# Gate logits of a two-layer decoder step: eight matmuls dealt out to four column groups of TensorE, and one matmul that adds their sums

## The reference, cut to what matters

```
z = jnp.einsum('btd,dn->btn', x, w_in) + b_in            # x: tokens x 1024
g_nsa = z[..., 1280:1304]                                # 24 of the columns: 8 heads x 3 branches
...
g = jax.nn.sigmoid(gl.astype(jnp.float32))               # gl = g_nsa
o = g[..., 0:1] * o_c + g[..., 1:2] * o_s + g[..., 2:3] * o_w
```

## Time and profile before

| | us |
|---|---|
| median of 3 runs | 1488.45 |
| lowest, highest | 1485.69, 1492.51 |
| the profiled execution, its own time | 1487.74 |
| its span, first to last instruction | 1486.0 |
| TensorE busy in the span | 1413.0 (95%) |
| VectorE busy | 342.0 (23%) |
| ScalarE busy | 307.9 (21%) |
| mean granted TensorE clock | 0.987 |

### The profile page before, as it was taken

The page is one execution under the profiler, slowest core; times in us unless marked ns, Lnnn a source line. Parts: engine busy times, 40 slices in busy tenths (PEclk is TensorE's granted clock), DMA queues, the critical chain, the costliest instruction groups (busy, mean ns, idle before and its releaser), DMA issues.

```text
span 1486.0 us, 23750 instructions
## 1 busy us (share of the span) xinstructions
PE 1413.0 (95%) x9098; PEld 1141.8 (77%) x9098; DVE 342.0 (23%) x887; ACT 307.9 (21%) x811; POOL 158.9 (11%) x268
## 2 busy tenths in 40 slices
PE   7999988999999999999999998899999999999996
PEld 4677767777769977777987777677776898777796
DVE  1222132344422311000122222324442221110002
ACT  1112242244310311000121223313432021100003
POOL 2100325000000000000300123420000000000000
PEclk9999999999999999999999999899999999999998
DMA  9999535596653666565945654467667447556640
GB/s 277 253 240 212 182 99 139 170 315 211 210 200 135 208 213 237 182 215 199 251 151 182 182 158 153 127 182 246 227 199 248 171 141 255 197 186 220 214 145 32
DMA packets 212771, 288.38 MB, mean 194 GB/s; under 512 B 14186, under 2 KB 201788, under 8 KB 211388
## 3 DMA queue, kind: packets, MB, share of 16 engines
q1 hardware_dynamic: 193573, 190.25, 42.8%
q10 hardware_dynamic: 9047, 71.53, 12.9%
q0 software_dynamic: 10048, 25.19, 6.4%
HBM read 277.03 MB, written 72.49 MB: 235 GB/s over the span
## 4 chain that ended last, share of the span: by engine, by line
PE 84%; SPq 5%; DMA 4%; DVE 3%; issue 2%; ACT 2%; DVEq 0%; ACTq 0%
PE psum L1632 76%; PE psum L1636 8%; DMA w_ring<-in_w_in 3%; SPq L506 1%; DMA yT<-in_cache_nsa_kv 1%; SPq L553 1%; SPq L578 1%; SPq L533 1%; SPq L521 0%; DVE pt L1503 0%; DVE logit L1394 0%; SPq L494 0%; SPq L501 0%; ACT xT L1213 0%; DVE logit L1559 0%
## 5 line engine op out<-in xcount | busy, mean ns | idle before, releaser
L1632 PE MATMUL psum<-arena,w_ring 128*128 128x144 f32 (+3 forms) x3584 | 679.5, 352 | 4.0 <-DVE arena L1610 2.3
L1632 PEld LDWEIGHTS psum<-arena,w_ring 128*128 128x128 f32 x3584 | 577.5, 190 | 106.7 <-issue 6.5
L1632 PE MATMUL psum<-xT,w_ring 128*128 128x288 f32 (+1 forms) x1472 | 362.4, 399 | 5.3 <-ACT kt L1152 3.1
L1632 PEld LDWEIGHTS psum<-xT,w_ring 128*128 128x128 f32 x1472 | 264.4, 190 | 79.5 <-issue 10.5
L1610 DVE TENSOR_TENSOR arena<-arena 128x288 f32 x64 | 29.3, 458 | 195.9 <-ACT arena L1225 195.9
L1225 ACT ACTIVATE arena<-psum 128x288 f32<-128x288 f32 x64 | 26.3, 411 | 193.3 <-PE psum L1632 193.3
L892 POOL TENSOR_TENSOR arena<-arena 128x144 f32<-128x144 f32 x24 | 11.7, 489 | 442.4 <-DVE arena L1605 441.3
L1636 PE MATMUL psum<-ident,regrouped 128*128 128x128 f32 x364 | 56.6, 287 | 1.8 <-ACT regrouped L945 1.4
L1636 PEld LDWEIGHTS psum<-ident,regrouped 128*128 128x128 f32 x364 | 45.0, 148 | 7.3 <-issue 3.2
L1306 DVE COPY arena<-psum 128x512 f32<-128x512 f32 x58 | 39.9, 690 | 32.4 <-PE psum L1636 30.7
L1614 DVE SCALAR_TENSOR_TENSOR arena<-arena,psum 128x288 f32<-128x288 f32 x12 | 4.9, 451 | 183.7 <-PE psum L1632 183.7
(11 more groups left out here) (248 smaller groups left out, 1170.8 us busy)
## 6 DMA issues: line engine op xcount, KB each, us to landing
w_ring<-in_w_ff SPq DMA_DIRECT2D x64, 1024.0 KB, 5.4
w_ring<-in_w_in SPq DMA_DIRECT2D x44, 1024.0 KB, 7.2
out<-in_cache_dil_w ACTq DMA_DIRECT2D x8, 1984.0 KB
w_ring<-in_w_o SPq DMA_DIRECT2D x8, 1024.0 KB, 7.7
out<-in_cache_nsa_win ACTq DMA_DIRECT2D x8, 992.0 KB
pages<-in_cache_nsa_kv POOLq DMA_DIRECT2D x32, 192.0 KB, 4.0
pages<-in_cache_nsa_kv SPq DMA_DIRECT2D x32, 192.0 KB, 5.1
arena<-in_cache_dil_w SPq DMA_DIRECT2D x46, 128.0 KB, 5.0
```

The source lines that it names most:

```text
L1632: return T.matmul(out, w, x, start=start, stop=stop, **kw)
```

## The change

The eight matmuls of the gate logits no longer accumulate in partitions 0 to 23 alone. Chunk k goes to the column group k mod 4, that is to partitions 32(k mod 4) to 32(k mod 4)+31 of bank 7; chunks 0 to 3 start the four partial sums, 4 to 7 complete them. The weights are loaded with 32 columns instead of 24. VectorE copies the four partial sums to SBUF (`gate_parts`), and after `z` tile 0 one more matmul with a matrix of ones at the right places (`gate_sum`, made once at the start) adds them in partitions 0 to 31 of bank 7. ScalarE waits for this second count of `g_mm`. `gate_w` moves from a tile of its own into a part of `pt`. Two semaphores that nothing waits for (`sp_steps` and `compute_steps`) become one, and `gate_parts_kept` is new.

```
-        sp_steps = ctx.enter_context(nc.semaphore("sp_steps"))
-        pool_steps = pe_steps = dve_steps = act_steps = ctx.enter_context(nc.semaphore("compute_steps"))
+        sp_steps = pool_steps = pe_steps = dve_steps = act_steps = ctx.enter_context(nc.semaphore("compute_steps"))
...
-        gate_w = sb("gate_w", [128, KC, 24])
+        gate_sum = sb("gate_sum", [128, 32])
+        gate_w = pt[:, :, :].rearrange("p a b -> p (a b)")[:, 512:768].rearrange("p (k n) -> p k n", k=KC)
+        gate_parts = logit[:, 576:576 + TOK]
...
-            queue.dma_start(gate_w[:, :, :], w_in[ld, :, GATE_COL:GATE_COL + 24]...
+            queue.dma_start(gate_w[:, :, :], w_in[ld, :, GATE_COL:GATE_COL + 32]...
...
@@ scalar
-                act.wait_ge(g_mm.sem, g_mm.after(l, 1))
+                act.wait_ge(g_mm.sem, g_mm.after(l, 2))
...
@@ vector, at the start
+            V.memset(gate_sum[:, :], 0.0)
...
+            dve.wait_ge(s_su_d.sem, 1)
+            for i in range(4):
+                V.tensor_copy(gate_sum[32 * i:32 * i + 32, 0:24], ident[32 * i:32 * i + 32, 32 * i:32 * i + 24])
...
@@ vector, in each layer, after the two instructions on prmc
+                dve.wait_ge(g_mm.sem, g_mm.after(l, 1))
+                V.tensor_copy(gate_parts, bank(7, 0, TOK)).then_inc(g_part.sem, 1)
...
@@ tensor
-                    last = mm(bank(7, 0, TOK, 0, 24), gate_w[:, k], xT[:, k], k == 0, k == KC - 1)
+                    rows = slice(32 * (k % 4), 32 * (k % 4) + 32)
+                    last = mm(bank(7, 0, TOK, rows.start, rows.stop), gate_w[:, k], xT[:, k], k < 4, k >= 4)
...
@@ tensor, after z tile i
+                    if i == 0:
+                        pe.wait_ge(g_part.sem, g_part.after(l, 1))
+                        mm(bank(7, 0, TOK, 0, 32), gate_sum[:, :], gate_parts).then_inc(g_mm.sem, 1)
```

More of the change, by code:

```diff
@@ L405, in build @@
         tm_t, tm_ev = sig("tm_transposed", 18), sig("tm_kept", 18)
-        g_mm, g_th, g_sg = sig("gate_logits", 1), sig("gate_tanh", 1), sig("gate_sigmoid", 1)
+        g_mm, g_part, g_th, g_sg = sig("gate_logits", 2), sig("gate_parts_kept", 1), sig("gate_tanh", 1), sig("gate_sigmoid", 1)
         g_t, g_row, g_st, g_ld = sig("gate_transposed", 1), sig("gate_rows", 1), sig("gate_stored", 16), sig("gate_loaded", 128)
@@ L479, in load_params @@
                 queue.dma_start(prm[R_LN + 8 * i:R_LN + 8 * i + 8], a[ld].rearrange("o (r n) -> (o r) n", n=128)).then_inc(prm_rdy.sem, 16)
-            queue.dma_start(gate_w[:, :, :], w_in[ld, :, GATE_COL:GATE_COL + 24].rearrange("o (k p) n -> p (o k) n", p=128)).then_inc(prm_rdy.sem, 16)
+            queue.dma_start(gate_w[:, :, :], w_in[ld, :, GATE_COL:GATE_COL + 32].rearrange("o (k p) n -> p (o k) n", p=128)).then_inc(prm_rdy.sem, 16)
             queue.dma_start(w2[:, :, :], cmp_w2[ld].rearrange("o c e d -> e (o c) d")).then_inc(prm_rdy.sem, 16)
```

## The result

The changed kernel took 1501.04 us, the median of 7 runs (1495.33 to 1502.71), against 1488.45 us for the kernel before (7 runs, 1485.63 to 1496.6). The ratio of the two groups of runs is 1.006, with a 95% interval from 1.0033 to 1.0088, so the loss is clear of the scatter. It is worked out from all the runs and need not equal the quotient of the medians, here 1.0085. The forecast was 1487.4, in a range from 1483 to 1492. The profiled execution took 1502.71, with a span of 1501.0, 15.0 us more than before.

What follows compares the result with a forecast made beforehand. TensorE, busy for 95% of the span, was taken to bound the kernel. Layer 1 (-1.96 + 0.83 + 0.1 = -1.0 us) plus layer 0 (0) took 1488.45 to 1487.4, range 1483 to 1492.

Steps and rivals of the forecast that it cites:

- 1.96 gained on the gate logits: Layer 1: next work at 758.30 instead of 760.26, with ScalarE's last chunks of `xT` as the limit; gain 1.96 us.
- The added matmul: Layer 1, after half of tile 0: two instructions, 0.49 us, plus 0.34 for entering and leaving, 0.83 us; VectorE's copy in time.
- the 0.34 that I charged for entering and leaving the narrow arrangement: Layer 1, added matmul: cost of changing arrangement, taken from `page_scores`, 0.77 less 0.43 us.
- The 0.1 us for 32 KB more of gate weights: Layer 1: the larger gate load lies ahead of the first weight unit and costs 0.1 us, bounds 0 and 1.0.
- Layer 0, TensorE's own side: Layer 0, tiles 0 and 1 end at 29.2 instead of 31.35, 2.1 us earlier, if the pace doubles at 22.03 again.
- I take all of this 2.1 as lost again: Layer 0, weight units before tile 8 and after: waits grow from 1.45 to about 3.5 us, net gain 0.
- the bound of +1: Layer 0: at most about 1 us lost if the earlier store of `toep_scratch` only displaces other transfers; other bound -2.1.
- The longer wait slows the clock: Layer 0, tiles 8 and 9: a 2.7 us wait brings a 1.7 us clock dip; 1488.3 to 1489.4; chance 0.22.
- its long form: Layer 0, tiles 8 to 11: low clock through all 64 instructions costs 15.5 us less 0.9; 1502; chance 0.02.
- Layer 0 keeps its gain: Layer 0: the landings move along and the 2.1 us stay won; -3.1 in all, 1485.3; chance 0.15.
- The groups don't work side by side: Gate logits, both layers: only costs stay, +0.9 us in layer 1, layer 0 hides its 0.83; 1489.4; chance 0.05.
- something unseen: Whole kernel: a time slower than 1495.9 needs this or the long clock dip; chance 0.05 for such a time.

Runs made afterwards that it cites:

- pad3: The changed kernel with three useless matmuls (6 instructions, 1.45 us) added behind tile 2 of layer 0: 1488.46 us, ratio 0.9995.
- windows_late: The changed kernel with the window keys of layer 0 loaded behind weight unit 8 instead of ahead of unit 4: 1479.97 us, ratio 0.9970.
- short_gates: The kernel before, without column groups, leaving out six of the eight chunks of the gate logits in layer 0: 1500.56 us, ratio 1.009.
- store_late: The changed kernel with the store of `toep_scratch` issued only when SyncE has issued weight unit 5: 1487.66 us, ratio 1.0009.
- pad6: The changed kernel with six useless matmuls (12 instructions, 2.9 us) added behind tile 2 of layer 0: 1483.21 us, ratio 0.9972.
- windows_half: The changed kernel with two of layer 0's four window loads left ahead of weight unit 4, two moved behind unit 8: 1490.37 us, ratio 1.0018.
- store_small: The changed kernel with the store of `toep_scratch` cut into three transfers of 128 columns, in packets of 512 bytes: 1497.38 us, ratio 1.0067.
- windows_late_before: The kernel before with the window keys of layer 0 loaded behind weight unit 8: 1482.88 us, ratio 0.9980.
- both_late: The changed kernel with layer 0's window keys behind weight unit 8 and the `toep_scratch` store held until unit 4 is issued: 1482.26 us, ratio 0.9961.

## Why the prediction was wrong, point by point

**Layer 1: right.** The forecast was 1.96 gained on the gate logits, measured 3.99 - 2.03 = 1.96, with ScalarE's chunks as the limit, as forecast. The added matmul was put at 0.83 and took 0.60; the 0.34 that I charged for entering and leaving the narrow arrangement, from `page_scores`, is 0.60 - 0.49 = 0.11 for a single pair. That is the term of layer 1 that was mis-sized. The Trainium skill's rule (TensorEngine Tiling (Array Packing), Key Properties) that a change of mode drains the engine agrees with a loss here, of 0.11 us only. No wait for `gate_parts` in the changed kernel (but one of 1.54 us in layer 0 of pad3's profiled execution), transposes 1.15 us sooner (forecast 1.1). The 0.1 us for 32 KB more of gate weights shows nowhere: the first weight unit of layer 1 was waited for 0.34 us, 0.84 before.

**Layer 0, TensorE's own side: right, slightly undersized.** 2.1 us gained by forecast, 2.90 by the time at which the store goes out. The slow pace ended sooner than the 22.03 that I carried over: tile 0 took 23.96 - 19.15 = 4.81 us.

**Layer 0, where the gain goes: the step that failed.** The prediction said of the 2.1 us "I take all of this 2.1 as lost again", and of the store of `toep_scratch`: "if this transfer only displaces others, about +1 (the size of the other waits, 0.64 + 0.22, rounded up). I take 0." Measured, tile 8 starts 14.72 us late, and tile 12, behind the slow clock, 15.57: the bound of +1 was passed by 14.6. Two faults are in this step. The bound has no ground: how late a load may come is not limited by how late it was before. And the store was laid beside unit 4, issued at 48.01, only 0.41 after it, and not beside what stands in SyncE's queue ahead of that unit: four window loads at 45.73 to 47.90. A shift of 2.1 us carries the store from 47.60 to 45.5, across the whole group. That was to be read from rows at hand: the store had 1.87 us to spare against the first window load, and the forecast shift was larger than that.

**The rivals.** "The longer wait slows the clock" named a true mechanism behind a wait of another cause and size: the granted clock was 0.59, 0.50 and 0.54 in the windows from 64 to 86 us, and cost 2.2 us, forecast 1.7. (Its upper bound of 1489.4 doesn't follow from its terms, which give 1487.4 + 1.7 = 1489.1.) That its long form gives 1502, close to the measured 1501, is luck: it put 15.5 us down to the clock, which took 2.2. "Layer 0 keeps its gain" holds once the collision is away: 2.7 us at tile 12 in windows_late. "The groups don't work side by side" is refuted by the 2.08 us at 17.07, at half pace. No rival had the mechanism that decided, which the prediction left to "something unseen". One of its signs of being wrong did fire: a difference over 7 us, for which none of its steps has room.

**What is shown and what is not.** Shown: the early store is enough for the loss (short_gates), and the loss goes when the store is held back (store_late), when TensorE is slowed (pad6) or when the loads in between are moved (windows_late); the loss grows with the loads in between (windows_half). Only argued: how the DMA engines divide their time. While SyncE's packets were in line first, its queue moved 2,700 packets in 8 us and the store 431; with the store first 838 and 650. Of this stretch the Trainium skill (DMA: Bandwidth & Descriptors, Queues, rings and completion order) says that each DMA engine goes round the queues that have work and changes after a packet. The near-equal counts of the changed kernel agree if a packet of the profile is one turn; the Trainium skill counts several descriptors as a packet there, and no run here shows whether the profile counts alike. The 2,700 to 431 of the kernel before and the 1,096 to 1,690 of store_small do not follow from it alone. Also open: whether the long executions of the kernel before itself (four of 23 beside pad3 lay between 1497.02 and 1500.08) are the same collision. None of them has a trace, but two things speak for it. SyncE's stream is not always on time: windows_late_before, which is the kernel before up to there, reached the place of the window loads at 47.59 instead of 45.73, with the store at 47.97, which would leave a lead of 0.4 us. And of the 34 runs of the three kernels with no window load ahead of unit 4 (windows_late, windows_late_before, both_late) none was above 1490.3, while of the 80 runs of the kernel before beside the experiments 15 were above 1494.

## What to carry to other kernels

Before an engine is made faster, list the transfers that are issued behind it, and the transfers of other queues between the old and the new moment of issue: every pair whose order would change is a risk with a price of its own, and the old waits are no bound for it. Here a transfer of 3,840 KB moved 2.9 us and cost 15.6 us by tile 12, and wasting those 2.9 us again won them back. If an order between two queues matters, write it down as a wait or move one of the two; don't leave it to the speed of a third engine.

## What I had not expected of the hardware

- A large store on one queue cut the other queue's rate to less than a third (2,700 to 838 packets in 8 us), although the same store, issued 1.87 us behind the other queue's first load instead of 1.52 ahead, let it run at 2,700. Loads of 256 KB landed after 8.3 to 19.5 us instead of 4.2 to 5.8.
- Together the two queues moved less: 1.56 MB (1.00 and 0.56) in those 8 us, against 2.33 (1.67 and 0.66). It was not the early store alone: with it and weights behind it (windows_late) they moved 2.05 (0.96 and 1.09).
- Issuing can hold the issuing engine's stream for long: four loads of 256 KB held SyncE's stream for 9.26 us instead of 2.17, and three stores held ScalarE's for 24.74, 0.96 for one.
